# The three passes of the split products, regrouped pass by pass over the outputs of a step

## What is computed

```
h    = modulate(rms_norm(x, g_mix), sh1, sc1)
proj = h @ w_in + b_in                    # 2048 -> 5376: rq rk rv rg aq ak av
ret  = retention(rq, rk, rv, rg)          # 4 heads of 256
att  = window_sink_attention(aq, ak, av, sinks)   # 16 heads of 64
x    = x + gt1 * (concat(ret, att) @ w_out)       # 2048 -> 2048
h    = modulate(rms_norm(x, g_ffn), sh2, sc2)
x    = x + gt2 * conv_glu(h, w_up, w_conv, b_conv, w_down)   # 2048 -> 11264, 5632 -> 2048
return modulate(rms_norm(x, g_final), f_shift, f_scale)
```

## Time and profile before

| | |
|---|---|
| device time, 3 runs | 1274.79, 1274.95, 1275.76 us; median 1274.95 us |
| span of the profiled execution, first to last instruction | 1273.8 us |
| mean granted TensorE clock, as a share of 2.4 GHz | 0.972 |
| PE busy | 1213.5 us, 95% |
| PEld busy | 1081.0 us, 85% |
| DVE busy | 936.9 us, 74% |
| ACT busy | 590.4 us, 46% |
| read from memory | 340.20 MB, mean 269 GB/s |

### The profile page before, as it was taken

How to read it: one execution, slowest core, us unless ns; L and a number is a source line. 1 busy time by engine, 2 the same in 40 slices (tenths; PEclk the granted TensorE clock), 3 DMA queues, 4 the chain that set the end, 5 groups by cost and what they waited for, 6 DMA issues and landing times.

```text
span 1273.8 us, 22235 instructions
## 1 busy us (share of the span) xinstructions
PE 1213.5 (95%) x7871; PEld 1081.0 (85%) x7871; DVE 936.9 (74%) x1106; ACT 590.4 (46%) x848; POOL 173.1 (14%) x293
## 2 busy tenths in 40 slices
PE   4877999999999998999999999999999999999995
PEld 2555989987888787999999999999999987887884
DVE  5786778789688895467777767777655575778886
ACT  3231636354335445644544445445454455545442
POOL 5543111111121120000100101000000001010000
PEclk8897999999899997999999999999999999999998
DMA  9999988788698994577878787877555456887851
GB/s 360 375 391 330 339 300 285 249 305 308 257 339 304 340 359 161 167 258 272 282 264 287 261 284 263 281 268 277 188 175 193 170 198 249 286 295 253 321 214 66
DMA packets 117092, 343.02 MB, mean 269 GB/s; under 512 B 9670, under 2 KB 12200, under 8 KB 116400
## 3 DMA queue, kind: packets, MB, share of 16 engines
q1 hardware_dynamic: 79232, 206.19, 46.7%
q0 software_dynamic: 37376, 134.30, 28.8%
q10 hardware_dynamic: 432, 1.84, 0.4%
HBM read 340.20 MB, written 2.10 MB: 269 GB/s over the span
## 4 chain that ended last, share of the span: by engine, by line
PE 85%; DVE 6%; DMA 5%; ACT 2%; issue 2%; POOL 1%; POOLq 0%; ACTq 0%; DVEq 0%
PE ps L1168 27%; PE ps L1170 26%; PE ps L1169 26%; DMA ada_raw<-in_w_ada 3%; DVE acc L750 2%; DMA arena<-in_w_ada 1%; DVE wlo L740 1%; PE ps L1211 1%; PE ps L1292 1%; DMA raw<-in_w_in 1%; PE ps L1304 0%; DVE xb L1020 0%; DVE arena L1018 0%; PE ps L1329 0%; PE ps L1220 0%
## 5 line engine op out<-in xcount | busy, mean ns | idle before, releaser
L1168 PE MATMUL ps<-hhi,whi 128*128 128x256 f32 x1824 | 523.7, 287 | 13.3 <-DVE wlo L740 10.4
L1169 PE MATMUL ps<-hlo,whi 128*128 128x256 f32 x1824 | 518.9, 284 | 0.0
L1170 PE MATMUL ps<-hhi,wlo 128*128 128x256 f32 x1824 | 518.8, 284 | 0.0
L470 ACT ACTIVATE whi<-raw 128x1024 fp32r<-128x1024 f32 x248 | 262.6, 1059 | 346.6 <-PE ps L1170 345.1
L745 DVE TENSOR_TENSOR wlo<-raw,whi 128x1024 fp32r<-128x1024 f32 x248 | 303.0, 1222 | 134.1 <-ACT whi L470 132.1
L1168 PEld LDWEIGHTS ps<-hhi,whi 128*128 128x128 f32 x1824 | 353.9, 194 | 32.4 <-issue 26.6
L1169 PEld LDWEIGHTS ps<-hlo,whi 128*128 128x128 f32 x1824 | 354.1, 194 | 0.0
L1170 PEld LDWEIGHTS ps<-hhi,wlo 128*128 128x128 f32 x1824 | 353.9, 194 | 0.0
L750 DVE SCALAR_TENSOR_TENSOR acc<-ada_raw,c_act,acc 128x1024 f32<-128x1024 f32 (+1 forms) x216 | 276.2, 1279 | 24.5 <-DMA ada_raw<-in_w_ada 20.6
L1168 PE MATMUL ps<-whi,hhi 128*128 128x512 f32 x608 | 242.4, 399 | 1.7 <-ACT arena L531 1.0
L1170 PE MATMUL ps<-whi,hlo 128*128 128x512 f32 x608 | 237.7, 391 | 0.0
(11 more groups left out here) (130 smaller groups left out, 637.5 us busy)
## 6 DMA issues: line engine op xcount, KB each, us to landing
raw<-in_w_up SPq DMA_DIRECT2D x176, 512.0 KB, 4.4
ada_raw<-in_w_ada POOLq DMA_DIRECT2D x160, 512.0 KB, 6.1
raw<-in_w_down SPq DMA_DIRECT2D x44, 1024.0 KB, 6.7
raw<-in_w_in SPq DMA_DIRECT2D x40, 1024.0 KB, 7.4
ada_raw<-in_w_final_ada POOLq DMA_DIRECT2D x64, 512.0 KB, 5.8
arena<-in_w_ada POOLq DMA_DIRECT2D x32, 512.0 KB, 9.6
raw<-in_w_out SPq DMA_DIRECT2D x16, 1024.0 KB, 7.7
xb<-in_x SPq DMA_DIRECT2D x2, 1024.0 KB, 6.2
```

Source lines behind the costliest of these rows:

```text
L470: nc.scalar.activation(whi[:, i % RING, :], raw_of(step0 + i), ACT.Copy).then_inc(hi_ready, 1)
L1168: nc.tensor.matmul(out_ap, lhs[0], rhs[0], start=start, stop=False, skip_group_check=skip)
L1169: nc.tensor.matmul(out_ap, lhs[0], rhs[1], start=False, stop=False, skip_group_check=skip)
L1170: return nc.tensor.matmul(out_ap, lhs[1], rhs[0], start=False, stop=True, skip_group_check=skip)
```

## The change

The three passes become the outer loop of a step. In `columns`, the first pass goes over the outputs in the first halves of the four banks, then over those in the second halves; then the second pass does the same, then the third. Within a pass a bank's two outputs are four matmuls apart, and any two consecutive matmuls write different banks. In `tokens`, the same is done for the two banks of each half of the tokens, so two banks take turns for six matmuls, then the other two. The matmuls are the same in number and in operands. The guards stay ahead of the first matmul into their bank, which in `columns` are now the first four matmuls of the step. For RG the order of banks becomes 1, 0, 2, 3. In a `final` step `out_ps` is counted up in the third pass. `keys_values` is as it was.

```diff
             def columns(slot, k, start, bank_of, cols=None, order=range(4), free=None):
-                for b in order:
-                    if free and free[b]:
-                        pe.wait_ge(*free[b])
-                    for m in (2 * b, 2 * b + 1):
-                        c0 = cols(m) if cols else slice(m * P, (m + 1) * P)
-                        last = passes(bank_of(b)[:, (m % 2) * S:(m % 2 + 1) * S],
-                                      (whi[:, slot, c0], wlo[:, slot, c0]), (hhi[:, k, :], hlo[:, k, :]),
-                                      start and m % 2 == 0, True)
+                for w, h, first in ((whi, hhi, True), (whi, hlo, False), (wlo, hhi, False)):
+                    for half in range(2):
+                        for b in order:
+                            if first and half == 0 and free and free[b]:
+                                pe.wait_ge(*free[b])
+                            m = 2 * b + half
+                            c0 = cols(m) if cols else slice(m * P, (m + 1) * P)
+                            last = nc.tensor.matmul(bank_of(b)[:, half * S:(half + 1) * S], w[:, slot, c0], h[:, k, :],
+                                                    start=start and first and half == 0, stop=w is wlo,
+                                                    skip_group_check=True)
                 last.then_inc(step_done, 1)

             def tokens(slot, k, start, bank0, order=range(4), free=None, final=False):
-                for n in order:
-                    if free and free[n]:
-                        pe.wait_ge(*free[n])
-                    t, b = n // 2, n % 2
-                    ts, cb = slice(t * P, (t + 1) * P), slice(b * 512, (b + 1) * 512)
-                    last = passes(ps[:, bank0 + n, :], (hhi[:, k, ts], hlo[:, k, ts]),
-                                  (whi[:, slot, cb], wlo[:, slot, cb]), start, True)
-                    if final and n < 3:
-                        last.then_inc(out_ps, 1)
+                for t in ((0, 1), (1, 0))[order[0] // 2]:
+                    ts = slice(t * P, (t + 1) * P)
+                    blocks = [n % 2 for n in order if n // 2 == t]
+                    for h, w, first in ((hhi, whi, True), (hhi, wlo, False), (hlo, whi, False)):
+                        for b in blocks:
+                            n = 2 * t + b
+                            if first and free and free[n]:
+                                pe.wait_ge(*free[n])
+                            last = nc.tensor.matmul(ps[:, bank0 + n, :], h[:, k, ts], w[:, slot, b * 512:(b + 1) * 512],
+                                                    start=start and first, stop=h is hlo, skip_group_check=True)
+                            if final and n < 3 and h is hlo:
+                                last.then_inc(out_ps, 1)
                 last.then_inc(step_done, 1)
```

## The result

| | before | changed |
|---|---|---|
| median of 13 runs each, in turns on one chip | 1274.79 us | 1278.80 us |
| lowest and highest | 1270.42 to 1279.49 us | 1276.49 to 1283.84 us |
| ratio, 95% interval | | 1.0044 (1.0028 to 1.0060) |
| span of the profiled execution | 1273.8 us | 1280.7 us |

The changed kernel is slower: 0.44% of 1274.79 is 5.6 us, with an interval of 3.6 to 7.6 us; the medians stand 4.0 us apart. The forecast was 6.0 us more. The execution profiled is one of the slower ones of the changed kernel: 1282.36 us, 3.6 above its median. In all runs whose span is on record the device time is some 1.7 us above the span, so the 1.15 us that stand before the prediction are not what lies around it; as the forecast adds differences to a median, it does not depend on this.

A forecast was written before the change was run, and what follows sets the result against it. From 157 us, the distance between matmul starts and PE's stops were taken to bound the kernel. 1274.95 + 4.5 (1.80 + 1.80 + 0.45 + 0.45) + 1.5 for the clock gave 1280.95 us; 8-in-10 range 1277.2 to 1283.9.

The forecast's parts named there:

- What bounds the kernel: From 157 us, the distance between matmul starts and PE's stops set the time; ACT and DVE wait for PE.
- RQ: First step: bank 0's guard leaves 21 matmuls behind the wait instead of six, +1.8 us.
- RK: First step: all four guards stand in the first four matmuls, so the last starts later, +1.8 us.
- RV: First step: four matmuls instead of two follow the last bank's opening, +0.45 us.
- The stream at nothing: Steady stream of 7200 matmuls: changing banks costs and gives nothing, 0 us, plus or minus 2 us.
- Rival 1: Same-bank accumulation costs 0.013 us a matmul; up to 94 us would go, about 1185 us; chance 0.05.
- the last step: The first bank's last pass is the fifth matmul, not the third, delaying DVE's residual, +0.45 us.
- The guards costed at nothing: RG, WO0, WO1, UP: no cost; without their lead, up to 0.45 us per `tokens` group, 1.4 us for all.
- The clock: Longer PE stops at RQ and RK lower the clock: one spell taken, +1.5 us, bounds nothing and 3 us.
- rival 4: The three first-step guard terms and the last-step term, without any low-clock spell: 1279.5 us; chance 0.25.

The follow-up runs named there:

- the bare guards' profile: Kernel before with the new order only in the seven guarded first steps: 1279.42 against 1272.83 us, ratio 1.0058.
- the first experiment: Kernel before with the new order everywhere except the guarded first steps and the two final steps: 1273.3 against 1272.83 us, ratio 1.000.
- RQ alone: Kernel before with the new order only in RQ's first step: 1277.89 against 1272.83 us, ratio 1.0054.
- keys first with the new order: Changed kernel with ACT's reads of keys and values moved ahead of one split of weights; against the kernel before 1278.38 to 1273.34 us, ratio 1.0048.
- guarded bank first: Kernel before, old order of passes, with RQ's banks in order 0, 1, 2, 3: 1277.52 against 1273.34 us, ratio 1.0037.
- filled: Changed kernel plus 15 overwritten matmuls each in RQ's and RK's waits; against the kernel before 1277.34 to 1272.83 us, ratio 1.0043; second look 1281.94 us.
- keys first with the old order: Kernel before with ACT's reads of keys and values moved ahead of one split of weights: 1273.27 against 1273.34 us, ratio 1.0002.

## Why the prediction was right

**What bounds the kernel** held: PE's stream, and PE's stops, with nothing behind them that catches up. What RQ and RK lost in the bare guards' profile was still there at RV.

**The stream at nothing** held to the hundredth in UP and DN, and for the time by the first experiment. The old trace had answered it: it held changes of bank and stays within a bank side by side, with equal distances. The 0.013 us a matmul that do not depend on the columns are not the price of writing one bank twice. What they are stays open; no run here varied the loads of the stationary operand. Rival 1's time should have read 1181 us, 1274.95 less 94, and not 1185.

**The guards.** RQ 1.80 foreseen, 1.79 measured; RK 1.8 and 1.76; RV 0.45 and 0.46; the last step 0.45 and 0.45 (DVE's wait 4.57 to 5.02). The experiment with the old order in the final steps had 4.56 there. RK's stops are 0.45, 0.27, 0.34 and 0.34 us; I had said 0.45 to 0.6, which the term did not use.

**The guards costed at nothing.** RG and WO1 cost nothing. WO0 cost 0.15 us. By the matmuls' starts it arose at the second guard: DVE's additions open the guards some 0.6 us apart, the new order asks for the second one matmul behind the first, and the third matmul started 0.77 us behind the first and not 0.64; from the fourth on the distances are even again. The bound of 0.45 us held.

**The clock.** I took one spell of 1.5 us. The trace after has two, at RQ (2.7 us, as it lasted some 6.8 us and not 3.4) and at RK (1.5 us). A spell of some 3.4 us cost 1.49 us in three places, as computed. Over ten profiles, a stop of some 2.2 us or more in RQ was followed by low clock in four of five (changed kernel, RQ alone, keys first with the new order, guarded bank first; not in the guarded steps alone), and one of 1.35 us or less in none of five (before, stream alone, filled twice, keys first with the old order). At RK one of three showed it, none of two when filled, which is too few to tell. The timed runs bear RQ's case out, since each lists its mean granted clock: 0.9723 on average over the 46 runs of the five kernels with such a stop, 0.9748 over the 86 of the others, with a standard error of 0.0004 each. Filling alone took it from 0.9722 (13 runs) to 0.9749 (12 runs), with a standard error of 0.0009 each. So the stop lowers the clock on average, though not in every execution. What that costs in time is an estimate: among runs of one kernel, 131 in all, 0.001 less of mean clock went with 0.54 us more, which makes 1.4 us for the 0.0025 between the two averages. The medians cannot show it: the filled kernel's ratio of 1.0043 is not below the changed kernel's 1.0044, and both have intervals wider than this.

**The size.** 1280.95 was forecast and 1278.80 measured, with 5.6 us by the ratio against the 6.0 forecast. The time alone does not choose between the forecast and rival 4, the four terms without a low spell: 1278.80 lies nearer to rival 4's 1279.45, and the interval of 3.6 to 7.6 us holds both sums. It is the profiles and the runs' clocks that speak for a spell. In the profiled execution the clock took 4.2 us and not 1.5; that its span grew by 6.9 us, near the 6.0 forecast, is in part luck, since 2.2 us came back in the three places that are not put down to the order. The medians of the variants, from 1.0037 to 1.0058, cannot be ranked; each interval is as wide as the differences.

None of the versions run is measurably faster than the kernel before.

## What to carry to other kernels

Before interleaving outputs to spare a resource, look in the old trace for places where the resource already changes hands; if the distance between starts is the same there, nothing is to be had. Then look at what the old order did besides: a loop turned inside out asks for all its outputs at once, so every wait on an output moves ahead of work that had covered it, and the price is the matmuls that move behind the wait, times their distance. Keep the old order in the few steps that have such waits, and where PE would stand still as long as here, 2.18 us and more, count the clock as well as the wait.

## What the runs showed of the hardware

- Float32r matmuls with their own load of the stationary operand start 0.120 us apart at 256 columns and 0.227 us apart at 512, at full clock, whether the next one writes the same bank, another half of it or another bank. The Trainium skill (TensorE: Matmul & The Clock Gate, Back-to-back issue gap) gives the gap of an isolated matmul as the columns over 2.4 GHz plus 2.5 ns, by estimate 0.109 and 0.216 us; the measurement decides here. At low clock it was 0.213 us for 256 columns.
- The clock fell with a stop of 2.18 us in one profile (keys first, new order), and did not with one of 3.13 us in another (guarded steps alone), with RQ's first step in the same order in both. In two profiles of one kernel, the filled one, the low spell after the 32 single-column matmuls of RV's last steps lasted 3.4 us and 6.8 us, and RQ was reached at 153.2 us and at 155.7 us. Over 131 runs, somewhat more than half of the variance between executions of one kernel goes with their mean granted clock (0.54 us for each 0.001), which limits what medians can tell.
- 30 extra matmuls put into PE's waits left the two first steps at 6.16 and 4.61 us, their lengths without them at full clock.
